# First attention of a two-block kernel: the mask goes into the score banks on TensorE, maximum and exponentials read PSUM

## The reference

```python
scores = einsum(q, k) * HEAD_DIM ** -0.5          # 8 query heads, 2 key heads, head width 64
scores = where(abs(qpos - kpos) <= 128, scores, -1e30)
probs  = softmax(concat([scores, sink]))[..., :-1]  # one sink logit per head
out    = einsum(probs, v)
```

## Time and profile before

| | |
|---|---|
| timed, median of 3 | 2967.48 us (2963.61 to 2970.08) |
| span of the profiled execution | 2767.7 us |
| its own time outside the span | not recorded; the median is 199.8 us above the span |
| TensorE busy | 2403.3 us, 87% of the span |
| VectorE busy | 2048.2 us, 74% |
| ScalarE busy | 768.7 us, 28% |
| GpSimd busy | 1067.3 us, 39% |
| first layer's attention | about 87 to 120 us |
| second layer's attention | about 919 to 952 us |
| bytes moved by DMA | 812.71 MB, mean 294 GB/s |

### The profile page before, as it was taken

How to read it: one execution, slowest core, us unless ns; L and a number is a source line. 1 busy time by engine, 2 the same in 40 slices (tenths; PEclk the granted TensorE clock), 3 DMA queues, 4 the chain that set the end, 5 groups by cost and what they waited for, 6 DMA issues and landing times. The chain is left out here.

```text
span 2767.7 us, 31616 instructions
## 1 busy us (share of the span) xinstructions
PE 2403.3 (87%) x9982; PEld 1616.9 (58%) x9982; DVE 2048.2 (74%) x3783; ACT 768.7 (28%) x1078; POOL 1067.3 (39%) x1124
## 2 busy tenths in 40 slices
PE   6988877787678999777778779999999999999998
PEld 4765333333235775333333336888878888888787
DVE  6986788788787876778778886667776646665765
ACT  3322011011012321100100114446543444445443
POOL 2326777777772337777777770002000000000000
PEclk9999988889999999999888889999999999999999
DMA  9689999999999789999999996664466655652564
GB/s 342 238 303 381 409 410 410 409 409 410 410 395 366 254 290 390 409 410 409 409 409 410 410 398 211 195 181 120 143 177 190 191 160 164 194 168 81 158 185 137
DMA packets 424192, 812.71 MB, mean 294 GB/s; under 512 B 26024, under 2 KB 262130, under 8 KB 424094
## 3 DMA queue, kind: packets, MB, share of 16 engines
q0 software_dynamic: 147968, 537.84, 49.1%
q1 hardware_dynamic: 276126, 273.62, 31.3%
HBM read 810.32 MB, written 1.05 MB: 293 GB/s over the span
## 5 line engine op out<-in xcount | busy, mean ns | idle before, releaser
L1822 PE MATMUL ps<-weight_ring,arena 128*128 128x512 f32 x1640 | 818.1, 658 | 258.3 <-PEq L1819 154.6
L1822 PEld LDWEIGHTS ps<-weight_ring,arena 128*128 128x128 f32 x1640 | 343.0, 213 | 727.8 <-issue 727.8
L2540 DVE CUSTOM_DVE_ANT_0 arena<-arena,ps 128x1024 f32<-128x1024 f32 x384 | 456.0, 1217 | 166.2 <-DMA arena<-in_peer_u,expert 147.2
L1460 PE MATMUL ps<-hT_pair,w_hi 128*128 128x512 f32 x1312 | 461.2, 396 | 6.1 <-PEq L1850 6.1
L2111 DVE TENSOR_TENSOR ring_lo<-weight_ring,w_hi 128x3072 fp32r<-128x3072 f32 (+1 forms) x102 | 325.4, 3191 | 170.7 <-DVEq L2110 170.7
L759 POOL DMA_INDIRECT weight_ring<-in_peer_v,expert x390 | 373.0, 956 | 121.1 <-issue 68.9
L753 POOL DMA_INDIRECT arena<-in_peer_u,expert x360 | 341.5, 949 | 131.5 <-issue 57.4
L1459 PE MATMUL ps<-hT_pair,ring_lo 128*128 128x256 f32 x1148 | 320.7, 279 | 0.0
L1460 PEld LDWEIGHTS ps<-hT_pair,w_hi 128*128 128x128 f32 x1312 | 240.8, 188 | 55.4 <-issue 8.5
L921 ACT ACTIVATE w_hi<-weight_ring 128x3072 fp32r<-128x3072 f32 (+1 forms) x102 | 267.8, 2626 | 8.5 <-ACTq L920 8.4
L1128 ACT ACTIVATE acts<-dots 128x8 f32<-128x8 f32 x64 | 13.2, 208 | 867.4 <-ACTq L1127 867.4
(11 more groups left out here) (400 smaller groups left out, 3959.9 us busy)
## 6 DMA issues: line engine op xcount, KB each, us to landing
weight_ring<-in_w_ada SPq DMA_DIRECT2D x48, 1024.0 KB, 7.4
weight_ring<-in_ffn_w_gate SPq DMA_DIRECT2D x88, 512.0 KB, 3.9
weight_ring<-in_ffn_w_up SPq DMA_DIRECT2D x88, 512.0 KB, 5.3
weight_ring<-in_ffn_w_down SPq DMA_DIRECT2D x88, 512.0 KB, 5.8
weight_ring<-in_peer_wq SPq DMA_DIRECT2D x16, 1024.0 KB, 9.2
weight_ring<-in_w_in SPq DMA_DIRECT2D x14, 1024.0 KB, 8.4
weight_ring<-in_rg_w_in SPq DMA_DIRECT2D x12, 896.0 KB, 5.2
weight_ring<-in_w_out SPq DMA_DIRECT2D x8, 1024.0 KB, 7.6
```

The costliest lines, as they stand in the source:

```text
L1460: ins = mm(both, w_high, s_pair, start=(k == 0), stop=last)
L1822: ins = mm(ps[:, 2 * t + c, :], diag[:, k, :], v_place(l, k)[:, c * N:(c + 1) * N], start=False, stop=False, skip_group_check=True)
L2540: ins = v.tensor_tensor_reduce(out=row, in0=row, in1=h_rows(t), scale=1.0, scalar=0.0, op0=ALU.mult, op1=ALU.add, accum_out=dots[:, g, j:j ...
```

## The change

The mask is added on TensorE: before a unit's scores, two matmuls with the identity as weights and the mask as moving operand write it into the two banks, in fp32r (one pass), and the scores accumulate on top in fp32. VectorE's maximum and ScalarE's exponentials read the banks themselves; the probabilities are written to `scores` in SBUF as before. VectorE's mask addition and `scores_taken` are gone. The banks are free again only when the exponentials have read them, so `score(2)` waits for `exps(0)` and `score(3)` for `exps(1)`. To have fp32r operands, `ident` and `window` are declared so and read elsewhere through an fp32 view, and the mask is built in `h_ext` and copied.

```diff
-        ident = sb("ident", [P, P])
+        ident_r = sb("ident", [P, P], F32R)
+        ident = ident_r[:].bitcast(F32)
-        window = sb("window_mask", [P, TILES, SEQ])
+        window_r = sb("window_mask", [P, TILES, SEQ], F32R)
+        window = window_r[:].bitcast(F32)
 # GpSimd, tables
-            g.memset(window[:], 0.0).then_inc(const_steps, 1)
+            mask = h_ext[:, 0:TILES * SEQ].rearrange("p (t s) -> p t s", t=TILES)
+            g.memset(mask, 0.0).then_inc(const_steps, 1)
...
+            pool.wait_ge(const_steps, build.next())
+            g.tensor_copy(window_r[:], mask).then_inc(const_steps, 1)
 # ScalarE, exps
                     for i in range(GROUP):
-                        ins = a.activation(scores[:, u % 3, i, :], scores[:, u % 3, i, :], ACT.Exp, bias=neg_max[:, u % 2, i:i + 1],
+                        logits = ps[:, WORK + 2 - 2 * (u % 2) + i // 2, i % 2 * SEQ:(i % 2 + 1) * SEQ]
+                        ins = a.activation(scores[:, u % 3, i, :], logits, ACT.Exp, bias=neg_max[:, u % 2, i:i + 1],
 # TensorE, score
-                    if u >= 2:
-                        pe.wait_ge(scores_taken, 1)
-                        pe.sem_inc(scores_taken, -1)
+                    for pair in range(2):
+                        mm(ps[:, WORK + 2 - 2 * (u % 2) + pair, :], ident_r[:], window_r[:, t:t + 1, :].to_broadcast([P, 2, SEQ]),
+                           start=True, stop=False)
                     for i, head in enumerate(heads):
                         ins = mm(ps[:, WORK + 2 - 2 * (u % 2) + i // 2, (i % 2) * SEQ:(i % 2 + 1) * SEQ], qTz[:, head, t * P:(t + 1) * P], kT,
-                                 start=True, stop=True)
+                                 start=False, stop=(i % 2 == 1))
 # TensorE, order
+                pe.wait_ge(probs_ready, 1)
                 score(2)
                 turn_probs(0)
+                pe.wait_ge(probs_ready, 1)
                 score(3)
...
-                pe.wait_ge(scores_taken, 1)
-                pe.sem_inc(scores_taken, -1)
                 out_rows(0, 1, start=True)
...
-                pe.wait_ge(scores_taken, 1)
-                pe.sem_inc(scores_taken, -1)
                 out_rows(0, 0, start=True).then_inc(slot_free[0], 1)
 # VectorE, first_rows
-                for pair in range(2):
-                    ins = v.tensor_tensor(scores[:, u % 3, 2 * pair:2 * pair + 2, :],
-                                          ps[:, WORK + 2 - 2 * b + pair, :].rearrange("p (i t) -> p i t", t=SEQ),
-                                          window[:, t:t + 1, :].to_broadcast([P, 2, SEQ]), ALU.add)
-                ins.then_inc(dve_steps, 1)
-                dve.wait_ge(dve_steps, steps.next())
-                dve.sem_inc(scores_taken, 1)
-                v.tensor_reduce(row_max[:, b, :], scores[:, u % 3], AX_X, ALU.max).then_inc(dve_steps, 1)
+                v.tensor_reduce(row_max[:, b, :], ps[:, WORK + 2 - 2 * b:WORK + 4 - 2 * b, :].rearrange("p g (i t) -> p (g i) t", t=SEQ),
+                                AX_X, ALU.max).then_inc(dve_steps, 1)
```

More of the change, by code:

```diff
@@ L370, in program @@
         scores_done = sem("scores_done")
-        scores_taken = sem("scores_taken")
         scores_ready = sem("scores_ready")
@@ L657, in _ @@
             pool.wait_ge(const_steps, build.next())
-            g.affine_select(out=ident[:], in_=zeros[:], compare_op=ALU.not_equal, fill=1.0, base=0,
+            g.affine_select(out=ident_r[:], in_=zeros[:], compare_op=ALU.not_equal, fill=1.0, base=0,
                             pattern=[[-1, P]], channel_multiplier=1).then_inc(const_steps, 1)
@@ L674, in _ @@
             pool.sem_inc(params_free, 1)
-            g.memset(window[:], 0.0).then_inc(const_steps, 1)
+            mask = h_ext[:, 0:TILES * SEQ].rearrange("p (t s) -> p t s", t=TILES)
+            g.memset(mask, 0.0).then_inc(const_steps, 1)
             pool.wait_ge(const_steps, build.next())
-            g.affine_select(out=window[:, 0, P:SEQ], in_=window[:, 0, P:SEQ], compare_op=ALU.is_ge, fill=MASKED,
+            g.affine_select(out=mask[:, 0, P:SEQ], in_=mask[:, 0, P:SEQ], compare_op=ALU.is_ge, fill=MASKED,
                             base=0, pattern=[[-1, P]], channel_multiplier=1).then_inc(const_steps, 1)
             pool.wait_ge(const_steps, build.next())
-            g.affine_select(out=window[:, 1, 0:P], in_=window[:, 1, 0:P], compare_op=ALU.is_ge, fill=MASKED,
+            g.affine_select(out=mask[:, 1, 0:P], in_=mask[:, 1, 0:P], compare_op=ALU.is_ge, fill=MASKED,
                             base=0, pattern=[[1, P]], channel_multiplier=-1).then_inc(const_steps, 1)
+            pool.wait_ge(const_steps, build.next())
+            g.tensor_copy(window_r[:], mask).then_inc(const_steps, 1)
             pool.wait_ge(const_steps, build.next())
```

## The result

The changed kernel took 2989.07 us in the median of five runs (2983.90 to 2992.66), the kernel before 2967.48 beside it; the ratio is 1.0065 (95% interval 1.0043 to 1.0088), which is 19 us slower (13 to 26). The prediction was 2977.7, or +10.2 us, with a range up to 2987.5. The first median lies 1.6 us above the top of that range; the differences that the two ratios give, 19 and 12 us, lie inside it.

What follows compares the result with a forecast made beforehand. VectorE's list was taken to bound the kernel around attention and carry shifts to the DMA-limited gathers. Per layer, 2.0 us for the loop plus 3.1 for low clock, twice, gave +10.2 on 2967.5: 2977.7 us, range 2965.5 to 2987.5.

Steps and rivals of the forecast that it cites:

- The path: VectorE's fixed list after attention: a shift at first_close(2) reaches the first gathers and the end, once per layer.
- The 199.8 us: Gap between profiled span 2767.7 and median 2967.48 us, taken as time outside the span and carried over unchanged.
- The loop: In attention, score(2) waits for exps(0), score(3) for exps(1), without overlap; 2.0 us late per layer at full clock.
- The clock: TensorE's idle holes bring half clock; score(2) and turn_probs(0) cost 3.1 us more, taken in both layers.
- VectorE's relief worth nothing: The 5.76 us a layer of mask addition removed from VectorE is eaten by its idle time.
- Mask matmuls near nothing off the loop: Two fp32r mask matmuls on TensorE cost 0.46 us a unit; costing nothing, they would make the full-clock loop 0.3.
- TensorE's tail at 0: Second layer's last output rows come 5 to 6 us later; slack of 3.3 us just holds, put at 0.
- The f32 price of a mask matmul: Upper bound for a 512-column mask matmul on TensorE: 0.44 us each, from sixteen plain f32 ones in 7.03 us.
- The full-clock case at the dear price: Attention loop without clock fall, mask matmuls at the f32 price: 7.7 us; 0.03 of chance counted as slower.
- The loop at full clock: Rival: the attention loop costs its time with no clock fall, +4.0 us, 2971.5; chance 0.19.
- The delay is not hidden: Rival claimed hiding: DMA sets the pace up to the gathers, its backlog absorbs 2 to 5 us, 2967.5; chance 0.12.
- The relief would count: Rival: VectorE's idle time stays under 5.76 us a layer, gain at best 11.5 us, 2956.0; chance 0.12.

Runs made afterwards that it cites:

- e1: The kernel before, run again with no edit, as a control; ratio 0.9994 (0.9977 to 1.0010).
- e11: The kernel before, unedited, once more on the same chip as e12; ratio 1.0005 (0.9993 to 1.0017).
- e4: The kernel before plus only the two mask matmuls per unit and fp32r tables, VectorE's mask addition kept; ratio 1.0011 (0.9998 to 1.0024).
- e6: The changed kernel plus matmuls of zeros in TensorE's holes, four before score(2) and three before score(3); ratio 1.0031 (1.0013 to 1.0049).
- e3: The kernel before plus only the two added waits of score(2) and score(3), mask addition kept on VectorE; ratio 1.0054 (1.0035 to 1.0073).
- e8: The changed kernel with turn_probs ahead of score(2) and score(3), added waits gone, modulation parts in VectorE's hole; ratio 1.0010 (0.9991 to 1.0028).
- e10: e8 plus three matmuls of zeros ahead of turn_probs(0) and the SCALE2 spread ahead of output rows (1, 0); ratio 1.0000 (0.9981 to 1.0019).
- e5: The changed kernel run again with no edit and more runs; ratio 1.0041 (1.0024 to 1.0059).
- e2: The changed kernel plus thirteen matmuls of zeros, seven before the wait of score(2), six before that of score(3); ratio 1.0075 (1.0048 to 1.0103).
- e12: e10 repeated on the same chip as e11; ratio 1.0000 (0.9985 to 1.0016).

## Why the prediction was right, point by point

The path, right in the first layer, and right in the second only in its sum. Against e1 `first_close(2)`, the gated addition and the first gather are late by 5.3, 5.7 and 5.8 us in the first layer, and by 5.7 each in the second. But e1 has a wait for the spread of SCALE2 in the second layer. Against e11, which has none, they are late by 5.8, 7.4 and 5.8 us: the wait for the spread adds 1.6, and the wait ahead of the choice of experts gives 1.7 back (3.03 us in e11, 1.34 in the changed kernel).

That last wait goes with TensorE's hole ahead of its keys and the clock behind it. Of the profiles with that hole in the second layer, the three with 2.46 to 2.94 us (the first one, e11, e4) have a stretch of half clock right behind it and a wait of 3.03 to 4.15, and the nine with 1.66 to 1.68 us have full clock there and a wait of 1.33 or 1.34. When the tail came later, the hole was shorter. The prediction had neither of the two; that they cancel is luck. Against the first profile of the kernel before, with its 4.15 us, the sum to the first gathers is 10.4 us and not 11.5.

The 199.8 us, wrong, without harm to the sum: I read them as time outside the span. e1 shows 1.7 us there and a slower pace of the gathers. I should have asked which stage of that profile could be 200 us too short, for a span and its own time differ little in every other profile here. The stages ahead of the gathers were sound in it: 115.17 - 87.41 is 27.76, in e1 27.79.

*The loop:* predicted +2.0 us a layer at full clock, measured +2.1 and +2.5 (e6). Its parts: `exps(0)` behind the copy of the spread, as put; from the start of the exponentials to TensorE 2.17 (94.64 to 96.81) instead of 2.30, so 0.13 less each where I took 0.035 per exponential, 0.14 for four; the pair of mask matmuls 0.46 to 0.65 where I had 0.46. The Trainium skill ("Perfetto Trace Analysis", Optimizing Scalar/DVE Operations) gives ScalarE an overhead some 40 ns smaller on PSUM than on SBUF; the trace agrees, 0.45 us from start to start against 0.49 in e1. It gives VectorE some 65 ns more on PSUM; here the maximum has 1.23 us against 1.22, which does not agree, and the measurement stands.

*The clock:* predicted +3.1 a layer, with one of the two scores at half speed. Measured 3.3 and 3.2, and 4.8 and 4.3 in the other profile. Size right, place not: both scores were slow, each by 1.1 to 1.3 us in the first profile of the changed kernel, with a return to 1.00 in between, where I had put the whole at `score(2)` and `turn_probs(0)`.

*VectorE's relief worth nothing:* right, and the step that e3 shows most plainly. *Mask matmuls near nothing off the loop:* right (e4, +0.2). *TensorE's tail at 0:* wrong. I looked at the last output rows, with 3.3 us of slack. The spread of SCALE2 stands ahead of them; in the first profile it ended at 961.64 and VectorE was ready for it about 962.6, so the slack there was 1.0 us. In the changed kernel the spread came 8.2 to 8.7 us later behind `score(0)`, and VectorE waited 2.05 us for it instead of 0.47.

*The f32 price of a mask matmul:* wrong, without harm. The sixteen of the earlier trace rows are records, two to a matmul, so a plain f32 matmul of 512 columns is 0.88 us and not 0.44, and a pair at that price 1.76. The full-clock case at the dear price would be about 14 us over both layers, 4.0 + 8 x 1.3, and not 7.7. The measured pairs ahead of the first three units, 0.47 to 0.65 us in the first layer, lie near the 0.46 of the sum.

The rivals. The loop at full clock is e6, a kernel and not this one. The delay is not hidden. The relief would count only if VectorE had something to do while the exponentials hold the banks: e8 gave it that, and met TensorE's list instead; with the clock kept up and the spread earlier (e10) the first gathers do come 7.5 us sooner in sum, and the time is the same.

What stays open is some 4 us. In the first difference it is more, so that 19 us were measured where the traces explain 11.5 and the forecast was 10.2. In ten of the eleven measurements of an edited kernel (all but e5) the time is 2.5 to 8 us above what the sum to the first gathers says: +19 against 11.5 for the first, +22 against 15.4 (e2), +16 against 13.5 (e3), +3.3 against 0.2 (e4), 0 against -7.5 (e10, e12). Each interval is 4 to 8 us to either side, several of them rest on the same runs of the kernel before, so that they are fewer than eleven independent findings, and the gather stages of one kernel differ by more between profiles (the second is 752.7 us in e1 and 765.8 in e11). The two gather stages together are 1514.4 to 1516.7 us in the profiles of e1 to e4, so in these four the excess is not there. It may be that a start of the gathers moved either way costs something; no run here shows where.

## What to carry to other kernels

Work taken off the fullest engine is a gain only if what replaces it doesn't lengthen the loop that feeds that engine: ask who holds the buffer now, and until when. Here a bank held until the exponentials had read it cost more than the 1.44 us per unit that VectorE saved, and two waits without any other edit cost as much as the whole change. Such a wait costs less where the engine behind it is given its work first (turn, then score), and an idle hole on TensorE can be paid twice, the second time in clock. Where a term is put at nothing for its slack, look for the first thing that the other engine asks for there, and not only the last. Set the span of a profile against that execution's own time before using it, and a stage that runs on DMA against a second profile.

## What the hardware showed that I had not expected

- The pace of the gathers can differ between profiled executions of one kernel: 410 GB/s in the first, 349 to 369 over 200 us in all others, 200 us in the whole. Whether it goes with the execution or with its chip is not on record.
- Two holes of TensorE, 3.20 and 2.79 us, each brought half clock for part of the next 6 us, and the clock was back at 1.00 between them. Matmuls of zeros in both holes kept it at 1.00 through the attention (e6).
- A plain f32 matmul of 512 columns takes 0.80 to 0.86 us at full clock (e2; the spreads) and shows as two records; an fp32r one has one record, and a pair takes 0.46 to 0.87 us at full clock, by what stands ahead of it.
- A gain of 7.5 us at the start of two gather stages gave none in the time, in two measurements that each could have told it, while losses of 11 to 14 us arrived in full.
